# Routing stage of a hybrid decoder layer: rank sums, gate matrix, bias and first gather put in another order

## What is computed

```python
def moe_ffn(h, router_w, router_b, w1, b1, w2, b2):
    logits = (ht @ router_w + router_b).astype(jnp.float32)
    top_val, top_idx = lax.top_k(logits, TOP_K)
    gates = jax.nn.softmax(top_val, axis=-1)
    ...
    order = jnp.argsort(flat_e)
    counts = jnp.bincount(flat_e, length=N_EXPERTS)
    ...
    def expert_block(args):
        idx, wt, e = args
        xb = h_pad[idx]
        u = xb @ w1[e] + b1[e]
        y = clamped_swiglu(u) @ w2[e] + b2[e]
        return y.astype(jnp.float32) * wt[:, None]
```

## Time and profile before

| | us |
|---|---|
| median of 3 runs | 1372.55 |
| lowest, highest | 1371.71, 1374.8 |
| profiled execution, its time | 1373.53 |
| profiled execution, span of the trace | 1371.4 |

### The profile page before, as it was taken

How to read it: one execution, slowest core, us unless ns; L and a number is a source line. 1 busy time by engine, 2 the same in 40 slices (tenths; PEclk the granted TensorE clock), 3 DMA queues, 4 the chain that set the end, 5 groups by cost and what they waited for, 6 DMA issues and landing times.

```text
span 1371.4 us, 28701 instructions
## 1 busy us (share of the span) xinstructions
PE 1202.2 (88%) x8815; PEld 432.0 (32%) x8816; DVE 459.9 (34%) x931; ACT 207.4 (15%) x469; POOL 280.4 (20%) x415
## 2 busy tenths in 40 slices
PE   4989997377999999999999997979798989898994
PEld 2433545222333333333333332213132323232231
DVE  3399544612223222223222222212122323222226
ACT  3124332001111111101111011101011111111111
POOL 3035001111132122221222212112121212221111
PEclk9999997589999999999999999989899999999996
DMA  9785515589166668899999999999999999999766
GB/s 339 279 292 213 228 56 215 227 329 417 53 264 257 270 266 338 352 366 418 392 419 415 410 420 419 419 421 418 420 419 421 419 420 419 411 409 419 323 234 272
DMA packets 80149, 462.83 MB, mean 337 GB/s; under 512 B 11922, under 2 KB 12066, under 8 KB 31488
## 3 DMA queue, kind: packets, MB, share of 16 engines
q1 hardware_dynamic: 52080, 314.72, 56.6%
q10 hardware_dynamic: 17568, 126.14, 22.3%
q0 software_dynamic: 10480, 21.71, 4.5%
HBM read 453.07 MB, written 16.91 MB: 343 GB/s over the span
## 4 chain that ended last, share of the span: by engine, by line
PE 67%; DMA 19%; DVE 9%; issue 3%; ACT 2%; ACTq 1%; SPq 0%; POOL 0%; DVEq 0%; POOLq 0%
PE bank L1603 33%; PE bank L1631 20%; DMA W<-in_expert_w 15%; PE bank L1509 4%; PE bank L1612 2%; DVE W L1027 2%; DMA W<-in_w_ada 2%; PE bank L1460 2%; PE bank L1591 1%; PE bank L1430 1%; DVE OV L1259 1%; DMA W<-y_rows 1%; PE bank L1392 1%; DMA store<-in_x 1%; PE bank L1558 0%
## 5 line engine op out<-in xcount | busy, mean ns | idle before, releaser
L1603 PE MATMUL bank<-W,OV 128*32 128x512 f32 x5056 | 560.6, 597 | 10.9 <-issue 10.8
L1631 PE MATMUL bank<-W,OV 128*32 128x512 f32 x2528 | 311.9, 628 | 62.3 <-DMA W<-in_expert_w 44.8
L1603 PEld LDWEIGHTS bank<-W,OV 128*32 128x32 f32 x5056 | 171.1, 111 | 378.6 <-issue 375.1
L1259 DVE TENSOR_TENSOR OV<-bank,OV 128x512 f32<-128x512 f32 x79 | 54.6, 692 | 367.2 <-PE bank L1603 361.6
L1272 DVE COPY OV<-bank 64x512 f32<-64x512 f32 x79 | 54.8, 693 | 306.6 <-PE bank L1631 304.5
L1631 PEld LDWEIGHTS bank<-W,OV 128*32 128x32 f32 x2528 | 76.2, 113 | 231.2 <-issue 160.7
L636 POOL DMA_INDIRECT OV<-h_rows,src_cur x104 | 106.4, 1023 | 61.1 <-POOL src_cur L631 44.2
L631 POOL COPY src_cur<-OV 128x2 int32 (+1 forms) x52 | 11.4, 220 | 433.7 <-PE bank L1591 399.7
L852 ACT ACTIVATE OV<-OV 128x256 f32<-128x256 f32 x79 | 35.4, 448 | 371.6 <-DVE OV L1261 368.3
L857 ACT ACTIVATE OV<-bank 128x256 f32<-128x256 f32 x108 | 41.5, 385 | 212.4 <-PE bank L1612 191.4
L1612 PE MATMUL bank<-ident,store 128*128 128x128 f32 x216 | 50.3, 315 | 16.5 <-DVE store L1267 15.2
(11 more groups left out here) (272 smaller groups left out, 759.6 us busy)
## 6 DMA issues: line engine op xcount, KB each, us to landing
W<-in_expert_w SPq DMA_DIRECT2D x252, 1024.0 KB
W<-in_expert_w ACTq DMA_DIRECT2D x120, 1024.0 KB
W<-in_w_ada SPq DMA_DIRECT2D x24, 1024.0 KB, 9.4
W<-y_rows SPq DMA_DIRECT2D x8, 1024.0 KB, 11.9
W<-in_w_in SPq DMA_DIRECT2D x2, 2048.0 KB, 12.8
W<-in_w_out SPq DMA_DIRECT2D x2, 2048.0 KB, 8.9
store<-in_x SPq DMA_DIRECT2D x4, 512.0 KB, 5.4
W<-in_w_in SPq DMA_DIRECT2D x2, 1024.0 KB, 16.2
```

What stands on the lines that cost most here:

```text
L1259: TTo(u_sb[:, hf, :], bank[hf][:, :], b1_cur, ALU.add).then_inc(u_ok[hf], 1)
L1603: last = mm(bank[hf][H * j:H * j + H, :], xT[:, hf, k % QM, H * (k // QM):H * (k // QM) + H], W1[:, slot, k, UW * j:UW * j + UW], start=(k ...
L1631: last = mm(bank[4 + hf][H * j:H * j + H, :], gT[:, hf, r, H * c:H * c + H], W2[:, c, r, HW * piece:HW * piece + HW], start=(c == 0), stop ...
```

## The change

1. TensorE: the rank sums, which stood ahead of the last logits, come behind the last total; the totals of the first three tiles come first.
2. VectorE: `route_tile(i - 2)` moves from behind tile i's norm to between its x1 and its norm. The memset of `counts` and the four constants come ahead of the last two tiles' routing. The gate matrix comes behind the indices and behind the two first selects.
3. SyncE: the upper half of the second expert's W1 waits for the gate matrix (`G_ok`) in place of `idx_ok`, since it overwrites that one's scratch.
4. GpSimd: the first gather takes its indices from `idx` directly, without a copy.
5. TensorE: the bias of the first expert is multiplied ahead of the first transposes.

```diff
-            sp.wait_ge(idx_ok, 1)
+            sp.wait_ge(G_ok, 1)
...
-            gather(0)
+            for hf in range(2):
+                pool.indirect_dma_start(xg[hf], None, h_rows,
+                                        bass.IndirectOffsetOnAxis(ap=idx[:, 0, 0, hf:hf + 1], axis=0),
+                                        bounds_check=T * J - 1, oob_is_err=False).then_inc(xg_in, 16)
+            pool.sem_inc(src_ok, 1)
...
                 TTo(x1[:, i, :], x1[:, i, :], m, ALU.add).then_inc(x1_ok, 1)
+                if i >= 2:
+                    route_tile(i - 2)
                 dve.wait_ge(x1_ok, i + 1)
...
-                if i >= 2:
-                    route_tile(i - 2)
             for j in range(J):
...
+            link(nc.vector.memset(counts[:, :, :].rearrange("p a e -> p (a e)"), 0))
+            dve.wait_ge(bias_const, 2)
+            link(TS(same_j.bitcast(i32), same_j.bitcast(i32), J - 1, None, ALU.bitwise_and))
...
             route_tile(TT - 2)
             route_tile(TT - 1)
...
-            link(nc.vector.memset(counts[:, :, :].rearrange("p a e -> p (a e)"), 0))
...
-            dve.wait_ge(top_exp, 1)
-            link(nc.vector.reduce_sum(top_d[:, :, 0], top_e, axis=AX.X))
...
-            dve.sem_inc(G_ok, 1)
...
             TTo(idx.rearrange("p v s h -> p v (s h)"), idx_f, over(idx_e, 1, P, 2, NQ), ALU.add).then_inc(idx_ok, 1)
             dve.wait_ge(idx_ok, 1)
 
+            dve.wait_ge(counts_ok, 4)
+            for i in range(2):
+                select(slice(i, i + 1), i)
+            dve.wait_ge(top_exp, 1)
+            link(nc.vector.reduce_sum(top_d[:, :, 0], top_e, axis=AX.X))
...
+            dve.sem_inc(G_ok, 1)
...
-                if what == ("logits", TT - 1):
-                    pe.wait_ge(route_const, 6)
-                    pe.wait_ge(bc_ok, 6)
-                    pe.wait_ge(sel_ok, TT - 1)
-                    for to in range(TT - 1):
-                        for b in range(to + 1):
-                            rank_add(to, b)
-                    for b in range(TT - 1):
-                        rank_add(TT - 1, b)
-                        total_add(b)
...
+            pe.wait_ge(sel_ok, TT - 1)
+            for b in range(TT - 1):
+                total_add(b)
             pe.wait_ge(sel_ok, TT)
             total_add(TT - 1).then_inc(rank_ok, 1)
-            rank_add(TT - 1, TT - 1).then_inc(rank_ok, 1)
+            for to in range(TT):
+                for b in range(to + 1):
+                    last = rank_add(to, b)
+            last.then_inc(rank_ok, 1)
...
-            transpose_x(0, first=True)
...
             pe.wait_ge(sel_e_ok, 1)
             mm(b1_bank[:, :], sel_e[:, 0, :], b1_all[:, :], start=True, stop=True).then_inc(b1_ps, 1)
+            transpose_x(0, first=True)
```

More of the change, by code:

```diff
@@ L1250, in _, with select @@
             dve.wait_ge(idx_ok, 1)
+            def select(i, slot):
+                e = dve.value_load(counts[0:1, 3, i], min_val=0, max_val=E - 1)
+                TS(sel_e[:, slot, :], same_j, hot_row[:, bass.ds(e, 1)], None, ALU.mult).then_inc(sel_e_ok, 1)
+            dve.wait_ge(counts_ok, 4)
[3 more added lines that the diff above has]
+            link(nc.vector.reduce_sum(top_d[:, :, 0], top_e, axis=AX.X))
+            link(nc.vector.reciprocal(top_d[:, :, 1], top_d[:, :, 0]))
+            link(TTo(gates[:, :, :], top_e, top_d[:, :, 1:2].to_broadcast([P, TT, TOPK]), ALU.mult))
+            spread = route_tmp.rearrange("p (i k) e -> p i k e", i=TT)
+            link(TTo(spread, hot_e, over(gates[:, :, :], 3, P, TT, TOPK, E), ALU.mult))
+            link(nc.vector.reduce_sum(G[:, :, :], spread.rearrange("p i k e -> p i e k"), axis=AX.X))
+            dve.sem_inc(G_ok, 1)
             def activate(hf, n, k):
@@ L1276, in finish @@
                 TTo(y_sb[hf], bank[4 + hf][0:YP, :], y_part[hf], ALU.add).then_inc(y_ok[hf], 1)
-            def select(i, slot):
-                e = dve.value_load(counts[0:1, 3, i], min_val=0, max_val=E - 1)
-                TS(sel_e[:, slot, :], same_j, hot_row[:, bass.ds(e, 1)], None, ALU.mult).then_inc(sel_e_ok, 1)
-            dve.wait_ge(counts_ok, 4)
-            for i in range(2):
-                select(slice(i, i + 1), i)
             dve.wait_ge(x1_stored, 16 * TT)
```

15 lines of the change are left out of this document (5 added, 10 removed).

## The result

The changed kernel takes **1365.62 us** (median of 22 runs, 1360.76 to 1376.81) against 1375.36 for the kernel before, run beside it 22 times (1371.71 to 1390.98). The ratio is 0.9930, 95% interval 0.9907 to 0.9953: a gain of 9.7 us, where 13.8 were forecast, and 1.6 us above the upper end of the range. The sign was right, the size was not. Two things make up the distance to 1358.7: the gain is 4.1 short, and the forecast was taken from 1372.55, the median of three runs of the kernel before, which is 2.8 under its median of 22.

A forecast was written before the change was run, and what follows sets the result against it. Bound taken: a serial thread of small steps up to the first up matmul, which sets the third expert's start. 6.45 + 0.21 + 2.80 + 0.35 + 3.5 + 0.5 = 13.8 us off 1372.55 gives 1358.7; range 1355 to 1364.

The forecast's parts named there:

- Logits, rank sums, top-4: Last logits no longer wait for rank sums, though a top-4 delays the norm: start from 234.90 to 228.42, 6.45 us taken.
- Gate matrix and constants (2.80), memset (0.21), copy (0.35): VectorE work and memset off the way to the indices, first gather without its index copy; us gained in brackets.
- Emptier queue: First gather falls into a gap between W1 loads and is waited for 2.4 us in place of 5.89: 3.5 us.
- Branch: TensorE's branch over the two-half code, ahead of the first up matmul, gets 0.5 us shorter; bounds 0 and 1.7.
- rival 4: Logits still wait, or the early arrival goes into a longer branch and half clock: about nothing left, 1372 us; chance 0.03.
- signs of being wrong: Transposes later than 261, branch over 2 us longer, or third expert's start moving less than the first up matmul.
- Clock in the first up matmuls: The granted clock may change at other moments during the first up matmuls: no gain or loss taken, 1.5 us either way.
- All of it carried past 319.7: The whole 13.8 us gained ahead of the third expert was to reach the kernel's end.
- the prediction's own losses: Bounds on what could be lost around the forecast: gather 3.5, branch 0.5, table 0.4, granted clock 1.5 us.
- the second: VectorE's selects and gate matrix hold up the gather's descriptors, landing 266.2, 7 us late: 1365.8 us; chance 0.06.
- The first: The weight stream, by bytes and not issue times, sets the third expert's start: 10.7 us gained, 1361.9; chance 0.10.
- The third: Clock left at half in the third expert; 40 us of it make the kernel slower, 1378.8 us; chance 0.03.

The follow-up runs named there:

- e5: The kernel before with only the rank sums behind the last totals and a tile's top-4 ahead of its norm; 1371.92 us, ratio 0.9969.
- e6: The changed kernel with the gate matrix ahead of the table again and SyncE waiting for the indices; 1370.02 us, ratio 0.9973.
- e1: The changed kernel with the second expert's upper W1 half issued only after the first expert used one chunk of its own; 1368.72 us, ratio 0.9945.
- e8: The changed kernel with the first expert's bias matmul behind the first transposes again; 1372.88 us, ratio 0.9944.
- e4: The changed kernel with eight empty instructions written ahead of the first transposes, left out by the build, so the same program; 1368.22 us, ratio 0.9946.
- e7: The changed kernel with eight empty instructions written behind the first transposes, left out by the build, so the same program; 1371.59 us, ratio 0.9947.
- e9: The changed kernel with 24 empty instructions written behind the first transposes, left out by the build, so the same program; 1371.64 us, ratio 0.9948.

## Why the prediction was wrong, and where it was right

The time is 6.9 us over the forecast. Of these, 2.8 are the base: with 1375.36 in place of 1372.55 the same range would have been 1357.8 to 1366.8 and would have held 1365.62. The other 4.1 are missing gain. At the third expert's start 2.1 of 13.8 us are missing (0.5 gather, 1.1 branch, 0.5 clock); the rest is lost behind it and in the shares of the two groups.

*Logits, rank sums, top-4 (6.45):* right. e5 shows 6.65 alone. The matmul of the places was 0.2 late as forecast (238.78) and cost nothing.

*Gate matrix and constants (2.80), memset (0.21), copy (0.35):* right in sum; the indices came at 254.43 for 254.40, the gathers at 255.40 and 256.82 for 255.3 and 256.75.

*Emptier queue (3.5):* 3.1, from 5.89 to 2.77 us. The gather was waited for 2.77 us, not 2.4; the transposes were 0.5 late. e6 confirms the mechanism.

*Branch (0.5 less):* **this step failed, in sign.** "Only its length can change, since loads ran beside it and now they are just restarting: I take 0.5 off." Transposes to first up took 7.07 to 8.39 us in the six traces of the changed program, against 6.70 and 6.76: 0.3 to 1.7 more, and 1.1 more than forecast in the first trace. The bounds, 0 and 1.7 won, left no room for a longer branch at all, though rival 4 and the signs of being wrong name one. The reason given, that loads lengthen the branch, is right (e1: 4.56 without them). But the loads restart at 260.5 and the branch stands from 260.31 to 266.45, full in them, with its code packet behind 263; before, the packet started at 276.19 and the loads thinned out at 276.5, under the second half of a branch from 273.3. The packet waited 3.75 us in place of 2.90, and that is the difference between the branches, 6.14 and 5.39. The prediction's own numbers put the end of the hole at 260.0 and the branch 0.8 behind 259.15: they met, and this wasn't drawn. The Trainium skill has the cause of such a stall (Runtime: NRT & Kernel Launch, "Instruction fetch mechanics"): a taken branch to code outside the pages at hand waits for a DMA fetch of that page. The traces agree: a 16 KB packet starts inside this branch wherever it takes over 3 us, in a DMA queue of its own (q8). Read with that page, the branch is a small DMA and belongs on the list of what the loads collide with.

*Clock in the first up matmuls (nothing, 1.5 allowed):* 0.8 lost. The granted clock stood at 0.50 from 254.7 to 271.8. Before, it had risen to 1.00 for 3.4 us behind 275.3, a stretch in which TensorE was busy for 0.03 us, and was at 0.50 again under the first up matmuls. The first row is the changed kernel's, the others are of the kernel before:

```profile
254.70:271.80 17.10, 8.02 (x30) 2.57 (x34) 3.01 (x8) 1.25 (x3) 6.75 (x9) 0.51 0.89 355
...
275.30:278.70 3.40, 0.03 (x1) 0.00 (x0) 0.28 (x1) 0.60 (x1) 1.49 (x2) 1.00 0.37 128
278.70:282.10 3.40, 2.89 (x16) 0.90 (x20) 0.00 (x0) 0.00 (x0) 0.00 (x0) 0.50 0.02 5
```

That the bias matmul's new place is to blame was tested by e8 and is not so. Nor is it the new order as such: the 64 records took 9.88 us in e5, which has the old order from the table on, and 8.50 in e6. What sets them is open.

*All of it carried past 319.7:* in the first pair of traces the third expert led by 11.7 us and the end by 7.6. Ahead of the up matmuls at 525.98 TensorE has 0.60 us of idle time that the kernel before did not have, and 2 more go in the last experts. In the second trace of the changed kernel the third expert led by 10.2, and the lead stayed between 9.2 and 10.7 to the end, 9.6. So of the same lead 4.1 us were given back in one execution and 0.6 in another, and the prediction had no term for it.

*The sum against the median:* the prediction took 1372.55 as the kernel's time and knew no second group. Within the groups the gain is 11.0 (1373.98 to 1362.94, medians of the lower ones) and 11.5 (1384.29 to 1372.81). The forecast less the three terms, 13.8 less 0.5 (gather), 1.1 (branch) and 0.8 (clock), is 11.4; that this is so near to 11.0 is in part luck, since it has nothing for what is given back late. The rest, down to 9.7, is that 10 of 22 runs of the changed kernel are in the upper group, against 8 of 22; its median is therefore nearer to that group. The three runs shown of the kernel before were all of its lower group. A range of 9 us for a kernel that has a 10 us step between its own runs was too narrow; and the prediction's own losses (3.5, 0.5, 0.4 and 1.5) add up to 5.9 us, which is 1364.6 and not 1364.

*The rivals:* the second's time (1365.8) is the nearest, by luck: the gather was not held up. The first (10.7, 1361.9) comes nearest in gain, by the wrong mechanism: the hole between the loads was too short for the bytes to decide, as e1 and e6 show. The third did not come: its stretch had the full clock, save 0.91 from 308 to 334. Half of the fourth did, "the early arrival is spent on a longer branch and a clock at 0.5", with 1.9 us and not the whole gain. Of the marks set for being wrong, the third expert's start moved by 11.7 where the first up matmul moved by 12.2, and that is what the text named.

## What to carry to other kernels

A jump over much code is a transfer: in a routing stage that starts weight loads just as TensorE or another engine enters its main loop, look for the branch's fetch among them, and give it a gap or something to be hidden under. Serial steps add up as read from the trace (12.9 of 13.3 us up to the transposes came as forecast), but the last stretch between the landing data and the first big matmul has terms of its own, branch and clock. Before forecasting to half a per cent, look at more than three runs: with two groups of times a change can move the shares as well as the groups. And before reading an experiment, compare its count of instructions with that of the kernel it was made from: e4, e7 and e9 were meant as three edits and are none.

## What was not expected of the hardware

- TensorE's entry to the third expert costs 5.2 to 7.5 us in some runs of a kernel and nothing in others, with 13 code packets of 16 KB in the queue in place of 6 from 240 to 460 us.
- Two to four matmuls whose result nobody reads, 50 us ahead of it, go with 0 of 25 runs above 1368 us, where the same program without them has 34 of 61.
- The branch over the two-half code ends 2.3 to 2.5 us behind the start of its 16 KB code packet, with the DMA engines full or idle; what varies is the packet's start, 1.03 us behind the branch's own without loads and up to 4.76 among them.
- Four idle matmuls behind the transposes brought the code packet ahead of the gather's landing, and the following 64 records ran in 7.07 us in both traces, at a granted clock that reached 1.00. The same four ahead of the transposes gave 7.07 once and 8.77 once.
- GpSimd's pass over the descriptors of a gather took 1.02 us beside the gate matrix's product and 1.12 beside two selects, against 1.01 alone.
